# A hybrid trunk on one core: three RMS norms taken in two halves of the tokens, the second feed forward's in column order

## What is computed

```
def rmsnorm(x, w):
    xf = x.astype(jnp.float32)
    xf = xf * lax.rsqrt(jnp.mean(xf * xf, axis=-1, keepdims=True) + EPS)
    return (xf * w.astype(jnp.float32)).astype(x.dtype)

def modulate(h, shift, scale):
    return h * (1.0 + scale) + shift
...
    for layer in range(DEPTH):
        hx = modulate(rmsnorm(x, norm_mix[layer]), mx[0], mx[1])
        hc = modulate(rmsnorm(ctx, norm_mix[layer]), mc[0], mc[1])
        ...  # layer 0: GLA and SSD heads; layer 1: mLSTM, scanned in column-major order of the grid
        x = x + mx[2] * (fx @ w_o)
        x = x + mx[5] * swiglu(modulate(rmsnorm(x, norm_ffn[layer]), mx[3], mx[4]),
                               ffn_w1[layer], ffn_w3[layer], ffn_w2[layer])
        if not last:
            ...  # the same for ctx, with mc
    return rmsnorm(x, final_norm)
```

## Time and profile before

| | us |
|---|---|
| median of three runs | 2336.34 |
| lowest, highest | 2332.36, 2336.76 |
| span of the profiled execution | 2333.6 |
| TensorE busy | 2265.1 (97%) |
| VectorE busy | 1373.3 (59%) |
| GpSimd busy | 1058.9 (45%) |
| ScalarE busy | 905.6 (39%) |

### The profile page before, as it was taken

How to read it: one execution, slowest core, us unless ns; L and a number is a source line. 1 busy time by engine, 2 the same in 40 slices (tenths; PEclk the granted TensorE clock), 3 DMA queues, 4 the chain that set the end, 5 groups by cost and what they waited for, 6 DMA issues and landing times.

```text
span 2333.6 us, 32704 instructions
## 1 busy us (share of the span) xinstructions
PE 2265.1 (97%) x11907; PEld 1956.1 (84%) x11907; DVE 1373.3 (59%) x1766; ACT 905.6 (39%) x1979; POOL 1058.9 (45%) x815
## 2 busy tenths in 40 slices
PE   7999999999889999999999999999999999999998
PEld 6999999998437999999999998976555567888887
DVE  5995878854676457756857456654478654211113
ACT  5215435443793356746746251232221213101002
POOL 3353335334442345544534434355243145776664
PEclk9999999999889999999999999999999999999999
DMA  8953334254531134534534423454233222333332
GB/s 278 312 164 114 108 117 150 80 179 143 190 117 37 55 102 132 146 106 120 153 100 132 83 75 118 128 168 141 67 117 104 68 69 76 99 98 92 99 97 84
DMA packets 392724, 281.07 MB, mean 120 GB/s; under 512 B 33442, under 2 KB 357820, under 8 KB 392604
## 3 DMA queue, kind: packets, MB, share of 16 engines
q1 hardware_dynamic: 334140, 202.43, 29.3%
q10 hardware_dynamic: 58464, 77.02, 9.7%
HBM read 237.34 MB, written 42.07 MB: 120 GB/s over the span
## 4 chain that ended last, share of the span: by engine, by line
PE 64%; DVE 5%; ACT 4%; issue 1%; DMA 1%; POOL 0%; ACTq 0%; DVEq 0%; SPq 0%; POOLq 0%
PE PS L967 46%; PE PS L1493 4%; PE PS L1691 4%; PE PS L1639 2%; PE PS L1505 2%; ACT Db L2086 1%; PE PS L1604 1%; ACT Dm L2093 1%; ACT Dm L2075 1%; ACT Dm L2078 1%; PE PS L1585 1%; DVE xcr L2553 1%; PE PS L1440 0%; PE PS L1427 0%; PE PS L899 0%
## 5 line engine op out<-in xcount | busy, mean ns | idle before, releaser
L967 PE MATMUL PS<-act_hi,w_hi 128*128 128x384 f32 (+1 forms) x1824 | 638.4, 350 | 5.2 <-ACT act_hi L1800 1.3
L967 PE MATMUL PS<-act_hi,w_lo 128*128 128x384 f32 (+1 forms) x1824 | 630.3, 346 | 0.0
L967 PE MATMUL PS<-act_lo,w_hi 128*128 128x384 f32 (+1 forms) x1824 | 627.0, 345 | 0.0
L749 POOL TENSOR_TENSOR w_hi<-w_raw,ones 128x128 fp32r<-128x128 f32 x232 | 128.3, 553 | 1041.0 <-DMA w_raw<-in_ffn_w 407.4
L752 POOL TENSOR_TENSOR w_lo<-w_raw,w_hi 128x1024 fp32r<-128x1024 f32 (+1 forms) x232 | 560.0, 2414 | 19.3
L967 PEld LDWEIGHTS PS<-act_hi,w_hi 128*128 128x128 f32 x1824 | 343.3, 188 | 28.1 <-issue 9.8
L967 PEld LDWEIGHTS PS<-act_lo,w_hi 128*128 128x128 f32 x1824 | 343.1, 188 | 15.5 <-issue 1.2
L967 PEld LDWEIGHTS PS<-act_hi,w_lo 128*128 128x128 f32 x1824 | 343.1, 188 | 13.5
L2168 ACT ACTIVATE fprod<-mf_ring,cs 128x128 f32<-128x128 f32 x896 | 267.9, 388 | 27.1 <-DVE mf_acc L2468 27.1
L2468 DVE TENSOR_REDUCE mf_acc<-fprod 128x128 f32<-128x1024 f32 x112 | 224.7, 2018 | 86.1 <-ACT fprod L2168 86.1
L750 POOL TENSOR_SCALAR w_hi<-w_raw 128x896 fp32r<-128x896 f32 (+1 forms) x232 | 235.2, 1014 | 0.0
(11 more groups left out here) (377 smaller groups left out, 3684.6 us busy)
## 6 DMA issues: line engine op xcount, KB each, us to landing
w_raw<-in_ffn_w SPq DMA_DIRECT2D x120, 512.0 KB, 4.1
mf_ring<-in_w_mod SPq DMA_DIRECT2D x56, 512.0 KB, 3.8
w_raw<-in_a_w_in SPq DMA_DIRECT2D x44, 512.0 KB, 4.3
proj<-stage ACTq DMA_DIRECT2D x44, 384.0 KB, 4.4
w_raw<-in_b_w_up SPq DMA_DIRECT2D x32, 512.0 KB, 4.6
m_ring<-in_w_mod SPq DMA_DIRECT2D x12, 1024.0 KB, 9.5
rows<-g_d SPq DMA_DIRECT2D x16, 768.0 KB
m_raw<-in_w_mod SPq DMA_DIRECT2D x4, 2048.0 KB, 11.8
```

The costliest lines, as they stand in the source:

```text
L749: pool.tensor_tensor(w_hi[:, s, 0], w_raw[:, s, 0], ones[:], ALU.mult)
L967: last = pe.matmul(to[:, c0:c1], w[:, s, k, :], x[:, k, c0:c1], start=k == 0 and w is w_hi and x is hi, stop=k == kt - 1 and w is w_lo)
```

## The change

At the norms ffn0, mix1 and ffn1 the tokens are taken in two halves (HALVES): 0 to 383 and 384 to 767 at ffn0, the context and then the latent tokens at mix1, and two halves of the column-major order, 256 and 256, at ffn1. There nacc, its squares, act and the whole second feed forward hold the tokens in column order (scaled reads x and the spread in row order of a half and writes column order; the feed forward's residuals read their products permuted).

- TensorE: tiles 6 and 7 of the last projection run half by half (end_in_halves): tile 6 and 7 on half 0, then tile 6 and 7 on half 1. The sums of half 0 stand inside tile 6's second half (behind k = 4, 3, 6 at the three norms), its spread inside tile 7's (behind k = 1, 1, 4). The idle products go.
- The next projection's first three tiles (begin_in_halves): half 0 with two tiles, the third joining at k = 3 with a wait for its weights; the sums of half 1 behind k = 4, its spread after k = 7; then half 1 with three tiles.
- VectorE (norm_in_halves) works 16 units, 8 for each half: scaled(u+1), act_lo(u); between the units of half 0 it has what half 1 needs: an addition after u = 0, tile 7's residual after u = 1, an addition after u = 3, reciprocal and diagonal after u = 5. ScalarE has tile 6's second square ahead of the units, tile 7's after u = 2, the root after u = 5.
- New buffers hnt and hnh, new counts half_done and half_evac (on semaphores in use elsewhere), sums and spreads in banks 6 and 7.
- tile 6's mm_done comes with its second half.

```diff
+        HALVES = {"ffn0": ((0, HALF), (HALF, T)), "mix1": ((LAT, T), (0, LAT)), "ffn1": ((0, LAT // 2), (LAT // 2, LAT))}
+        NORM_DIAGONALS = {"up00": GLA_HEADS + 4, "xm": GLA_HEADS + 5 + ("ffn0" in HALVES),
+                          "up10": GLA_HEADS + ML_HEADS + 6 + ("ffn0" in HALVES) + ("mix1" in HALVES)}
+        SUMS_AT = {"ffn0": (4, 4), "mix1": (3, 4), "ffn1": (6, 4)}
+        SPREAD_AT = {"ffn0": 1, "mix1": 1, "ffn1": 4}
...
+            def end_in_halves(name, seg, kt, operand):
+                n = segs[seg][0]
+                for h in range(2):
+                    for m in (KD - 2, KD - 1):
+                        if h == 0:
+                            pe.wait_ge(w_split, n + m + 1)
+                            pe.wait_ge(evac, n + (3 if m == KD - 2 else 5))
+                        for k in range(kt):
+                            done = half_products(end_half(name, m, h), m % RING, k, kt, *operand(k, h))
+                            if k == kt - 1:
+                                done.then_inc(mm_done if h else half_done, 1)
+                            if h and m == KD - 2 and k == SUMS_AT[name][0]:
+                                half_sums(name, 0)
+                            if h and m == KD - 1 and k == SPREAD_AT[name]:
+                                half_spread(name, 0)
...
+            def begin_in_halves(name, seg):
...
+                for k in range(1, KD):
+                    pe.wait_ge(act_ready, ready + k + 1)
+                    for s in (0, 1):
+                        step(s, k, 0)
+                    if k == 3:
+                        pe.wait_ge(w_split, n + 3)
+                    if k >= 3:
+                        step(2, k - 3, 0)
+                    if k == SUMS_AT[name][1]:
+                        half_sums(name, 1)
+                half_spread(name, 1)
+                for k in range(KD - 3, KD):
+                    step(2, k, 0)
+                pe.wait_ge(evac, n)
+                for k in range(KD - 2):
+                    pe.wait_ge(act_ready, ready + KD + k + 1)
+                    for s in range(3):
+                        step(s, k, 1)
+                for s in range(3):
+                    for k in (KD - 2, KD - 1):
+                        pe.wait_ge(act_ready, ready + KD + k + 1)
+                        done = step(s, k, 1)
+                    done.then_inc(mm_done, 1)
...
-            norm_products("ffn0", T)
+            if "ffn0" in HALVES:
+                second_out_tiles(KD - 2)
+                end_in_halves("ffn0", "out1", KD, all_rows("ffn0", act_hi, act_lo))
...
+            def norm_in_halves(name, n, layer, which, permute=False):
+                squares(name, n)
+                half_square(name, KD - 2)
+                half_square(name, KD - 1)
+                root(HALVES[name][0][1] - HALVES[name][0][0], D, 3, at=bank(6), q0=HALVES[name][0][0] // P)
+                half_square(name, KD)
+                for u in range(2 * KD):
...
+                    if u == 2:
+                        half_square(name, KD + 1)
+                    if u == 5:
+                        root(HALVES[name][1][1] - HALVES[name][1][0], D, 3, at=bank(7), q0=HALVES[name][1][0] // P)
...
+                def scaled(u):
+                    k, h = u % KD, u // KD
+                    c0, c1 = HALVES[name][h]
+                    if u >= 2:
+                        dve.wait_ge(nh_done, nh_count(name, u - 1))
+                    dve.tensor_tensor(half_view(name, hnt[:, u % 2, 0:c1 - c0]), x_half(name, k, h), half_view(name, spread_bank(name, h)),
+                                      ALU.mult).then_inc(nt_done, 1)
...
+                half_diagonal(name, 0)
+                half_residual(name, seg, KD - 2, 1, layer, which)
+                dve.wait_ge(rstd_done, rstds[0])
+                scaled(0)
+                for u in range(KD):
+                    if u + 1 < KD:
+                        scaled(u + 1)
+                    low(u)
+                    if u == 0:
+                        add_norm_square(name, KD, n)
+                    elif u == 1:
+                        half_residual(name, seg, KD - 1, 1, layer, which)
+                    elif u == 3:
+                        add_norm_square(name, KD + 1, n)
+                        dve.drain().then_inc(sum_done, 1)
+                    elif u == 5:
+                        half_diagonal(name, 1)
```

More of the change, by code:

```diff
@@ new lines, in before @@
+        def before(names, name, count):
+            return sum(count(x) for x in names[:names.index(name)])
+        STAGES = ["mix0", "gla", "ssd", "ffn0", "mix1", "ml0", "ml1", "ffn1"]
+        READY = {name: before(STAGES, name, lambda x: norm_units(x)) for name in STAGES}
+        NT0 = {name: before(NORMS, name, norm_units) for name in NORMS}
+        SQ0 = {name: before(NORMS[1:], name, lambda x: len(square_units(x))) for name in NORMS[1:]}
+        NSUM0 = {name: before(NORMS[1:], name, lambda x: len(square_units(x)) - 1) for name in NORMS[1:]}
@@ new lines, in nh_count, with x_half, half_view @@
+        def nh_count(name, units):
+            parts = lambda x, n: sum(len(unit_parts(x, u)) for u in range(n))
+            return before(NORMS, name, lambda x: parts(x, norm_units(x))) + parts(name, units)
+        def x_half(name, k, h):
+            c0, c1 = HALVES[name][h]
+            if name == "ffn1":
+                return xT[:, k, 0:LAT].rearrange("p (r c) -> p r c", c=GRID_W)[:, :, c0 // GRID_H:c1 // GRID_H]
+            return xT[:, k, c0:c1]
+        def half_view(name, ap):
+            return ap.rearrange("p (c r) -> p r c", r=GRID_H) if name == "ffn1" else ap
@@ L1374, in _, with second_out_tiles, half_products @@
             project_unit("out1", n0 // RING, 3, KD, act_hi, act_lo, T, act_ready, READY["ssd"])
-            each_ring(pe, n0 + RING, RING, lambda r, s: project_unit("out1", r, s, KD, act_hi, act_lo, T, act_ready, READY["ssd"]))
+            def second_out_tiles(count):
+                for m in range(RING, count):
+                    project_unit("out1", n0 // RING + 1, m - RING, KD, act_hi, act_lo, T, act_ready, READY["ssd"])
+            def half_products(out, s, k, kt, hi, lo, passes=(0, 1, 2)):
+                for i in passes:
+                    w, x = ((w_hi, hi), (w_hi, lo), (w_lo, hi))[i]
+                    last = pe.matmul(out, w[:, s, k, :], x, start=k == 0 and i == 0, stop=k == kt - 1 and i == 2)
+                return last
@@ L1723, in _ @@
                 last.then_inc(mm_done, 1)
-            for m in range(3, KD):
+            for m in range(3, KD - 2 if "ffn1" in HALVES else KD):
                 pe.wait_ge(w_split, n0 + m + 1)
@@ L2910, in ffn @@
                             scales(1, which)
+                    if layer == 0 and g == 2 and "mix1" in HALVES:
+                        norm_in_halves("mix1", "down02", n, 0, 5)
+                        continue
                     residual(f"down{layer}{g}", layer, 5, n, then=None if g < 2 else ("mix1", "final")[layer],
-                             late=layer == 0 and g < 2)
-            norm("ffn0", T)
+                             late=layer == 0 and g < 2, permuted=layer == 1 and "ffn1" in HALVES)
+            if "ffn0" not in HALVES:
+                norm("ffn0", T)
             ffn(0, T)
-            norm("mix1", T)
+            if "mix1" not in HALVES:
+                norm("mix1", T)
             dve.wait_ge(m4_done, 1)
```

248 lines of the change are left out of this document (208 added, 40 removed).

## The result

The changed kernel takes 2345.22 us (median of 6 runs, 2342.53 to 2352.54) where the kernel before takes 2335.45 (6 runs): a ratio of 1.0046, 95% interval 1.0034 to 1.0059, so 8 to 14 us slower. The forecast was 2338 with a range to 2345; the case that came is the slower one, that had 0.26.

A forecast was written before the change was run, and what follows sets the result against it. TensorE bounds the kernel, holding 64% of the chain of waits. -35.6 + 7.2 + 1.6 + 24.6 + 1.3 + 0.6 + 1.7 = +1.4 us on 2336.34 gave 2338, range 2327 to 2345.

The forecast's parts named there:

- the slower one: Case that the granted clock falls in most begin stages: 2343 us, range 2341 to 2349, chance 0.26.
- What bounds, and where the gain sits: At the three norms, stretches without useful products were all the change could win: 35.6 us, 1.5% of the span.
- the stalls: TensorE waiting in the next projection's first tiles: 7.4 us at ffn0, 9.1 at mix1, 8.1 at ffn1, together 24.6.
- The clock: One fall to 1.2 GHz of 3.3 us in the three stages, losing half: 1.7 us; bounds 0 and 10.
- The second rival: Clock falls in most begin stages: four falls of 3.3 us instead of one, 5.1 us more, 2343; chance 0.26.
- The splits: VectorE additions or subtractions held by POOL's w_lo: one collision a norm, 2.0 to 2.1 us, 6.1 in all.
- its rival: No collisions and no clock fall: queues stall 17.9 us instead of 24.6, giving 2330; chance 0.23.
- The start of the second half: TensorE waits there for scaled, nh, act_hi and hand-overs: 1.7 us at ffn0, 2.75 at mix1, 1.25 at ffn1.
- Products of 256 columns: At ffn1 120 products become pairs of about 0.12 us each: 1.6 us added, bounds 0 and 4.
- The fifth tile of up10: Tile 4 of up10 waits longer for w_lo because tile 0 frees its slot later: 1.3 us more, bounds 0 and 1.3.
- Strided operands: At ffn1 VectorE's scaled writes column order: 0.13 us a unit, 0.6 us showing; bounds 0 and 2.5.
- ScalarE's squares of tiles 0 to 5 in column order: Priced at nothing because ScalarE sat idle 4.8 us before one; without that cover 0.56 us each.

## Why the prediction missed, point by point

- *What bounds, and where the gain sits:* right. The stretches without products vanished, and the time came back as waits in the stage behind them, named by VectorE's subtraction at units 1 to 3, as said, and at unit 4 at ffn0. At the second half's start they name the subtraction too (below), not ScalarE's act_hi. Taken together the stalls were not put in too low: 24.6 us, where TensorE's idle time by the profile is 22.2 in the three stages.
- *The clock:* the step that failed most. One fall, 1.7 us, was put in for the three stages, with full clock at ffn0 and mix1; there were 17.1 us at the lower clock. The fall at ffn0 alone cost 3.2 us beside the same waits without one, and filling the waits gave 3.1, 1.5 and 0.3 us back. The second rival named this mechanism and 2343. The argument against it, that the trace of before holds the full clock at ffn0 and mix1, was one execution: mix1 without halves has a fall in three of five traces, two of them with w_lo in pieces.
- *The splits:* the other term that was too small, at ffn1. One collision a norm was put in, 2.0 to 2.1 us, 6.1 in all (its rival took off 6.7 for them; the parts add up to 6.1). There were three long ones at ffn0 (4.0 us), yet they cost the path 2.1 us there, and 1.1 to 2.2 at mix1. So the count was wrong and the size right at these two, by luck: the other stalls came out smaller (the 0.95 at ffn0's unit 5 did not show as a wait). At ffn1 they cost 3.5 to 4.3 us where 2.0 were put in: w_lo of the second tile of up10 runs beside the additions ahead of the sums, the next one beside the addition ahead of unit 1. The bounds, 0 to 4.7 a norm, did hold this.
- *The range* ended at 2345 and the median is 2345.22. The two bad cases were priced apart, each as a rival of its own, and here they came together.
- *ffn0 and mix1 otherwise:* with the clock held (idle products) they give 1.0 and 0.7 us against before; the sum had 1.6 and 1.1 (12.51 + 0.35 - 2.7 - 9.1). With short splits they give 3.2 and 1.4.
- *The start of the second half:* 1.7 and 2.75 us were worked out for ffn0 and mix1. TensorE's time line has 0.2 us less in each:

```profile
816.24 0.41 PE L1455 MATMUL PS<-act_hi,w_hi 128*128 128x384 f32 x1 [1.49 <-DVE act_lo L2787]
...
1377.44 0.47 PE L1455 MATMUL PS<-act_hi,w_hi 128*128 128x512 f32 x1 [2.53 <-DVE act_lo L2787]
```

- *Products of 256 columns:* starts lie 0.12 us apart at full clock, as the line through the rows gave; at 1.2 GHz 0.21 (TensorE's time line):

```profile
1955.37 0.41 PE L1455 MATMUL PS<-act_lo,w_hi 128*128 128x256 f32 x1
1955.58 0.41 PE L1455 MATMUL PS<-act_hi,w_lo 128*128 128x256 f32 x1
...
1956.90 0.28 PE L1455 MATMUL PS<-act_hi,w_hi 128*128 128x256 f32 x1
1957.02 0.28 PE L1455 MATMUL PS<-act_lo,w_hi 128*128 128x256 f32 x1
```

  The estimate of 0.109 by the rule of the Trainium skill ("TensorE: Matmul & The Clock Gate", section "Wait — 56ns, not 53.3ns?"), columns over 2.4 GHz plus 2.5 ns, was not reached.
- *The fifth tile of up10:* 1.3 us were added to the 0.31 of the earlier trace rows. Measured:

```profile
1994.03 0.47 PE L1039 MATMUL PS<-act_hi,w_hi 128*128 128x512 f32 x1 [1.56 <-POOL w_lo L819]
```

- *Strided operands:* 0.13 us a unit was taken, 0.23 measured, near the upper end of 0.28. The Trainium skill ("SBUF — State Buffer", the note on cachelines), by which an access that crosses to a new 16-byte line pays, spoke for that end, and the trace agrees with 0.645 us against 0.414. What it costs in the whole is 1.1 to 1.7 us by the stages, not settled by the timing; 0.6 was put in.
- *ScalarE's squares of tiles 0 to 5 in column order* were put at nothing behind 4.8 us of idle time. They take 1.20 us instead of 0.63, and ScalarE sat idle 13.1 us before three of them:

```profile
L1968 ACT ACTIVATE nsq<-xT 128x512 f32<-128x512 f32 x3 | 3.6, 1201 | 13.1 <-DVE xT L3065 13.1
```

## What to carry to other kernels

Before work is moved into a stage because its engine has slack there by busy time, list what else runs in that stage on an engine that can block it, instruction by instruction, and price the meetings by the longest single instruction of the other engine; then work out which of them the path waits for. At ffn0 three hits cost the path what one had been priced at; at ffn1 they cost about twice that. A long instruction of a helper engine can be cut into pieces: w_lo in four instructions cost GpSimd 3 us more at each norm and took 11.7 us off the kernel. The granted clock is a case of its own in the forecast: 6.2 us of waits at ffn0 came once with a fall and once without, 3.2 us apart, so both cases want a price, and stages are compared at a like clock, those of the kernel before too.

## What was not expected of the hardware

The hold works both ways, and also with w_hi, which reads one operand. At mix1, VectorE's addition of 512 columns and POOL's w_hi:

```profile
1359.15 0.96 DVE L2738 TENSOR_TENSOR nacc<-nacc,nsq 128x512 f32<-128x512 f32 x1
...
1359.53 1.38 POOL L817 TENSOR_SCALAR w_hi<-w_raw 128x896 fp32r<-128x896 f32 x1
```

An addition of 512 columns took 0.72 us in the earlier trace rows, w_hi 0.94 (the one from 796.98 above, beside which the subtraction from 797.00 took 1.32). The first part of w_hi (L816, which reads two operands) ran from 1359.10 to 1359.57 here, beside the addition's start. VectorE's multiplication that reads PSUM (scaled, 794.53 above) lasted its usual 0.54 us beside a w_lo: of the instructions read here, only those with both inputs in SBUF were held.
